# Softmax layers of a six-layer fp32 block on one core: copies moved ahead of exponents, filler and split positions changed, some low parts moved to GpSimd

## The reference, cut to what matters

```python
def dsa_mixer(xn, positions, w_in, q_norm, k_norm, w_out):      # the sparse layer
    q, k, v, z, qi, ki, wi = split(xn @ w_in)
    q = rope(rmsnorm(q, q_norm)); k = rope(rmsnorm(k, k_norm))  # 16 heads of 64
    rel = relu(einsum("qhd,sd->qhs", qi, ki)); score = einsum("qh,qhs->qs", wi, rel)
    top_val, top_idx = top_k(where(chunk_visible, score, -inf), 64)
    p = softmax(q . k[top_idx] * 64 ** -0.5)
    return ((p . v[top_idx]) * silu(z)) @ w_out

def mla_mixer(...):                                             # the latent layer
    cq, ckv, kr, z = split(xn @ w_in)
    q = rmsnorm(rmsnorm(cq) @ w_uq); kv = rmsnorm(ckv) @ w_ukv  # 16 heads of 96
    o = softmax over visible chunks (q . k * 96 ** -0.5) . v
    return (o * silu(z)) @ w_out
```

## Time and profile before

| what | us |
|---|---|
| median of 3 runs | 994.96 |
| lowest, highest | 992.82, 998.03 |
| profiled execution | 992.32 |
| its span, first to last instruction | 990.5 |
| PE busy within the span | 925.2 |
| DVE, ACT, POOL busy | 640.2, 500.1, 313.5 |
| mean granted TensorE clock | 0.974 |

### The profile page before, as it was taken

One profiled execution on the slowest core, in us unless ns is written; L12 is line 12 of the kernel. 1 busy time (PEld: TensorE's weight loads), 2 busy tenths in 40 slices (PEclk: granted clock), 3 DMA queues, 4 the chain that ended last, 5 costly groups with the idle time before them and its releaser, 6 DMA issues.

```text
span 990.5 us, 16827 instructions
## 1 busy us (share of the span) xinstructions
PE 925.2 (93%) x6793; PEld 867.7 (88%) x6793; DVE 640.2 (65%) x1006; ACT 500.1 (50%) x700; POOL 313.5 (32%) x270
## 2 busy tenths in 40 slices
PE   5999999988878997989999999899999999999988
PEld 5999987668667986769999999899999998988987
DVE  5776665896574788864677666678556544655642
ACT  5534455454574676674443353434535336575632
POOL 6433322342013225122443336965203000223320
PEclk9999999998999998999999999899999999999998
DMA  9886444344014425316386444253663752424401
GB/s 248 207 208 192 159 170 170 107 149 170 31 58 144 168 66 186 115 41 170 110 231 191 170 171 155 101 204 136 255 218 126 246 185 86 167 89 171 170 1 43
DMA packets 123170, 148.20 MB, mean 150 GB/s; under 512 B 9521, under 2 KB 79070, under 8 KB 123102
## 3 DMA queue, kind: packets, MB, share of 16 engines
q1 hardware_dynamic: 122384, 146.16, 45.6%
q0 software_dynamic: 464, 1.02, 0.4%
q10 hardware_dynamic: 254, 0.07, 0.0%
HBM read 146.18 MB, written 1.05 MB: 149 GB/s over the span
## 4 chain that ended last, share of the span: by engine, by line
PE 60%; DVE 8%; ACT 7%; POOL 3%; issue 2%; DVEq 0%; ACTq 0%; POOLq 0%
PE acc L1618 43%; PE aux L1618 16%; DVE wlo L862 2%; ACT whi L464 1%; POOL arena L1473 1%; ACT work L657 1%; ACT arena L490 1%; POOL arena L1474 1%; POOL arena L1472 1%; ACT whi L456 1%; ACT work L664 1%; ACT work L655 1%; DVE score L1110 1%; DVE arena L969 1%; DVE top L1109 1%
## 5 line engine op out<-in xcount | busy, mean ns | idle before, releaser
L862 DVE TENSOR_TENSOR wlo<-raw,whi 128x2048 fp32r<-128x2048 f32 (+5 forms) x118 | 281.3, 2410 | 104.2 <-ACT whi L456 102.5
L1618 PE MATMUL acc<-xh,whi 128*128 128x256 f32 x1128 | 323.7, 287 | 7.7 <-DVE wlo L862 4.2
L1618 PE MATMUL acc<-xl,whi 128*128 128x256 f32 x1128 | 320.9, 285 | 0.0
L1618 PE MATMUL acc<-xh,wlo 128*128 128x256 f32 x1128 | 320.8, 284 | 0.0
L456 ACT ACTIVATE whi<-raw 128x2048 fp32r<-128x2048 f32 (+5 forms) x118 | 202.9, 1748 | 86.5 <-PE aux L1618 45.3
L1618 PEld LDWEIGHTS acc<-xh,whi 128*128 128x128 f32 x1128 | 218.0, 193 | 9.9 <-issue 5.8
L1618 PEld LDWEIGHTS acc<-xl,whi 128*128 128x128 f32 x1128 | 218.1, 193 | 0.0
L1618 PEld LDWEIGHTS acc<-xh,wlo 128*128 128x128 f32 x1128 | 217.8, 193 | 0.0
L1618 PE MATMUL acc<-whi,xh 128*128 128x512 f32 (+1 forms) x208 | 82.6, 397 | 7.9 <-DVE arena L969 4.0
L1537 POOL CAST yh<-ytmp 128x256 fp32r<-128x256 f32 x24 | 16.9, 705 | 217.4 <-DVE ytmp L1393 123.3
L1618 PE MATMUL aux<-yh,whi 128*128 128x256 f32 x288 | 81.9, 284 | 0.0
(11 more groups left out here) (331 smaller groups left out, 1757.2 us busy)
## 6 DMA issues: line engine op xcount, KB each, us to landing
raw<-in_a_w_in SPq DMA_DIRECT2D x52, 512.0 KB, 6.7
raw<-in_sb_w_in SPq DMA_DIRECT2D x48, 512.0 KB, 5.6
raw<-in_b_w_in SPq DMA_DIRECT2D x36, 512.0 KB, 5.4
raw<-in_pool_w_in SPq DMA_DIRECT2D x32, 512.0 KB, 5.7
raw<-in_a_w_out SPq DMA_DIRECT2D x16, 512.0 KB, 4.9
raw<-in_pool_w_out SPq DMA_DIRECT2D x16, 512.0 KB, 5.1
raw<-in_sb_w_out SPq DMA_DIRECT2D x16, 512.0 KB, 5.0
raw<-in_a_w_in SPq DMA_DIRECT2D x16, 256.0 KB, 5.6
```

The lines of the kernel that those rows point to most:

```text
L862: TT(wlo[b][:, lo:hi], (raw_third if third else raw[b])[:, lo:hi], whi[b][:, lo:hi].bitcast(F32), ALU.subtract).then_inc(lo_ready, 1)
L1618: return nc.tensor.matmul(out_, lhsT, rhs, start=start, stop=stop, skip_group_check=True)
```

## The change

Ten edits, in the sparse and the latent layer.

- `root(1)` uses logarithm and exponent (`log=True`) in place of a square root, and B0+2's first half is split in two quarters on ACT and on DVE, with the root between ACT's quarters.
- DVE's second `top64` moves behind `half_factor(1)`, just ahead of `take(B0 + 7, ...)`.
- The low part of B0+8 moves from DVE (two halves) to POOL (four quarters, `weights_low`). POOL scales the last two k rows (rope 8 and 9) only after that; ACT splits B0+8 around `half_root(1)`.
- ACT copies transposed heads in pairs, at odd steps, ahead of that step's exponents.
- Filler positions: B0+9 at 5, 7, 8, 9 (were 6 to 9), C0+7 at 5, 7, 8, 9 (were 5, 6, 8, 9).
- C0+7 is split by quarters at steps 2 to 5, C0+8 at 8 to 11 (was 2 to 5), C0+9 at 12 to 15 (was 11 to 14).
- The table load inside `softmax_heads` is made once, ahead of the sparse layer's call.
- `turn_heads(15)` goes to psum bank acc 0, which the first PV uses; that PV waits for `turn_copy(15)`.
- In the q loop ACT's `log_root` for k stands ahead of the squares, and DVE's split of C0+5 and C0+6 behind the sums of c = 0 and c = 1.
- DVE's `turn_copy` 5 to 11 stand ahead of `q_factor(0)`.

```diff
-        MLA_SPLITS = {first + q: (u, q) for first, u in ((2, C0 + 8), (11, C0 + 9)) for q in range(4)}
+        MLA_SPLITS = {first + q: (u, q) for first, u in ((2, C0 + 7), (8, C0 + 8), (12, C0 + 9)) for q in range(4)}
...
-            return (acc[:, 1, :], acc[:, 2, :], acc[:, 3, :], acc[:, 1, :])[i - 12]
+            return (acc[:, 1, :], acc[:, 2, :], acc[:, 3, :], acc[:, 0, :])[i - 12]
...
-            split(B0 + 2, (0,))
+            split_quarter(B0 + 2, 0)
+            root(1, log=True)
+            split_quarter(B0 + 2, 1)
...
+            split(B0 + 8, (0,))
             half_root(1)
+            split(B0 + 8, (1,))
             token_out(3)
-            split(B0 + 8)
...
+                    if i % 2 and i > 1:
+                        for h in (i - 3, i - 2):
+                            act.wait_ge(sem("pt_psum"), h0 + h + 1)
+                            if h >= 2:
+                                act.wait_ge(sem("pv_done"), h0 + h - 1)
+                            A(work[:, 2 + h % 2, :], aux[:, 2 + h % 2, 0:W384], ACT.Copy)\
+                                .then_inc(sem("pt_ready"), 1)
                     if i < HEADS:
...
-                    if 2 <= i <= HEADS + 1:
-                        h = i - 2
...
-            split(C0 + 7)
             softmax_heads(1)
...
-            top64(P, W384)
             split(B0 + 7, (0,))
             token_turn(4)
             token_sums(4)
             half_mean(1)
             split(B0 + 7, (1,))
             half_factor(1)
-            split(B0 + 8)
+            top64(P, W384)
             take(B0 + 7, 24, "z_raw")
...
+            def weights_low(u, q, signal):
+
+                c = slice(1024 * q, 1024 * q + 1024)
+                pool.wait_ge(hi_ready, 2 * u + 1 + q // 2)
+                TT(wlo[u % 2][:, c], raw[u % 2][:, c], whi[u % 2][:, c].bitcast(F32), ALU.subtract).then_inc(signal, 1)
+
             for j in range(10):
                 token_rope(j)
+            pool.wait_ge(lo_ready, 2 * (B0 + 8))
+            for q in range(4):
+                weights_low(B0 + 8, q, lo_ready if q % 2 else sem("low_quarter"))
+            pool.wait_ge(sem("k_turned"), 2)
+            pool.wait_ge(sem("hfB_ready"), 2)
+            for j in (8, 9):
+                f = hf[:, 1, 1, HEADS * (j % 2) + 8:HEADS * (j % 2) + 16]
+                TT(by_head(raw_slot(j)), by_head(raw_slot(j)), f.rearrange("p (h d) -> p h d", d=1).broadcast_to([P, 8, 64]),
+                   ALU.mult).then_inc(sem("tok_done"), 1)
...
-                if 6 <= f < 10:
-                    if f == 6:
+                if f in (5, 7, 8, 9):
+                    if f == 5:
                         taken("v_ready", 4)
-                    unit(B0 + 9, in_tiles(1), xh, xl, part=(2 * (f - 6), 2))
+                    unit(B0 + 9, in_tiles(1), xh, xl, part=(2 * (5, 7, 8, 9).index(f), 2))
...
-                    unit(C0 + 7, in_tiles(1), xh, xl, part=(2 * (5, 6, 8, 9).index(f), 2))
+                    unit(C0 + 7, in_tiles(1), xh, xl, part=(2 * (5, 7, 8, 9).index(f), 2))
...
+                        if layer == 1 and t == 0:
+                            taken("turn_out_v", 8)
```

More of the change, by code:

```diff
@@ L547, in _ @@
             split(B0 + 1)
-            root(1)
             nc.scalar.preload_act_table_set("natural_log_exp_and_others")
@@ L677, in softmax_heads @@
                         nc.scalar.preload_act_table_set("natural_log_exp_and_others")
+            nc.scalar.preload_act_table_set("natural_log_exp_and_others")
             softmax_heads(0)
@@ L755, in _ @@
                 A(qraw[2 * g][:, h:h + 4, :], src, ACT.Copy).then_inc(sem("q_out_a"), 1)
+                if c == 0:
+                    log_root(c_heads(0, 1, 1), c_heads(1, 1, 1), "k_ms", 2, "k_root")
                 for t in range(NT):
@@ L1024, in _ @@
             split(B0 + 1)
-            factor(1, spread=False)
-            split(B0 + 2, (0,))
+            factor(1, spread=False, log=True)
+            split_quarter(B0 + 2, 0)
+            split_quarter(B0 + 2, 1)
             dve.wait_ge(sem("tab_ready"), 12)
@@ L1167, in softmax_heads @@
                         ins.then_inc(sem("p_ready"), 1)
+                    if layer == 0 and i == 4:
+                        dve.wait_ge(lo_ready, 2 * (B0 + 8) + 2)
                     if layer == 0 and i - 2 in SPARSE_SPLITS and i - 2 < 14:
@@ L1173, in softmax_heads @@
                         q_factor(1)
-                    if layer == 1 and i - 2 in MLA_SPLITS and i - 2 < 13:
+                    if layer == 1 and i - 2 in MLA_SPLITS and i - 2 < 14:
                         split_quarter(*MLA_SPLITS[i - 2])
+            dve.wait_ge(sem("picked"), 2)
             softmax_heads(0, pick, 24)
@@ L1265, in _ @@
                     ins.then_inc(sem("k_ms"), 1)
-            split(C0 + 5)
             for c in range(4):
@@ L1284, in _ @@
                     TS(c_heads(0, 0, g), c_heads(0, 0, g), 1 / 96, EPS, ALU.mult, ALU.add).then_inc(sem("q_ms"), 1)
-                if c == 1:
-                    split(C0 + 6)
+                if c < 2:
+                    split(C0 + 5 + c)
                 if c == 2:
@@ L1289, in _ @@
                     turn_copy(3)
+            for i in range(5, 13, 2):
+                turn_copy(i)
             q_factor(0)
-            turn_copy(5)
-            turn_copy(7)
-            turn_copy(9)
-            turn_copy(11)
-            split(C0 + 7)
             softmax_heads(1, mask, 40)
@@ L1522, in token_rope @@
                 ins = TT(raw, raw, turn, ALU.add)
-                if e in (2, 4):
-                    g = e // 2 - 1
+                if e == 4:
+                    ins.then_inc(sem("k_turned"), 1)
+                    return
+                if e == 2:
+                    g = 0
                     me.link(ins)
@@ L1544, in attention_low @@
                     if t in (4, 5):
-                        c = slice(1024 * (t - 2), 1024 * (t - 2) + 1024)
-                        pool.wait_ge(hi_ready, 2 * u + 2)
-                        TT(wlo[u % 2][:, c], raw[u % 2][:, c], whi[u % 2][:, c].bitcast(F32), ALU.subtract)\
-                            .then_inc(lo_ready if t == 5 else sem("low_quarter"), 1)
+                        weights_low(u, t - 2, lo_ready if t == 5 else sem("low_quarter"))
             pool.wait_ge(sem("turned"), 10)
@@ L1898, in mla_filler @@
                     turn_heads(13 + 2 * f)
-                if f in (5, 6, 8, 9):
+                if f in (5, 7, 8, 9):
                     if f == 5:
```

5 lines of the change are left out of this document (1 added, 4 removed).

## The result

The changed kernel takes **1000.3 us** (median of 8 runs, 999.3 to 1001.5); the kernel before, on the same chip, 994.7 (8 runs, 990.8 to 998.0). The ratio is 1.0058, with a 95% interval of 1.0039 to 1.0077: slower by 5.6 us, where 994.4, a range from 984.5 to 1000.0 and "no change" were forecast. The profiled execution of after has a span of 999.3 us and a time of 1001.45.

A forecast was written before the change was run, and what follows sets the result against it. PE was taken as busy nearly throughout, the two softmax stretches as chains between engines. Terms -3.3 + 5.9 - 1.0 - 2.2 gave -0.6 us, so the median went from 994.96 to 994.4, range 984.5 to 1000.0.

The forecast's parts named there:

- A: Start of B0+2: PE starts 1.7 us earlier and the clock is kept, 1.6 us more; -3.3, bounds -3.3 and -1.7.
- B: B0+7 and B0+8: first gap goes, but POOL's quarters delay DVE's half_factor, top64 and take; +5.9, bounds -5.1 and +6.5.
- C: Sparse softmax, from PE's first filler to the output product: -1.0 us, bounds -2 and +1.5.
- worse case: Sparse filler 5: the clock falls in PE's wait, so the transposes of pair 2 come at 269.4 instead of 268.1.
- D: Latent layer: first logits 5.5 us sooner, partly lost at filler 5 and to ACT; -2.2, bounds -4 and +1.9.
- low case: Latent filler 5 half at the low clock: scores of pair 3 at 406.8 instead of 405.3, giving -0.7.
- That order is unchanged: End of sparse softmax: ACT's last high quarter, POOL's 2.38 us, its two parts, gate and last PV still follow in turn.
- Rival 3: Both softmax layers: filler 5's 24 matmuls at 1.2 GHz delay needed scores; sum +5.0, median 1000.0 to 1001.6; chance 0.14.

The follow-up runs named there:

- e9: The kernel before with only the new start of B0+2 (root by logarithm and exponential, split by quarters): 992.1 us, ratio 0.9987.
- e12: Changed kernel with GpSimd's quarters behind half_factor, both fillers at 6, GpSimd's later low quarters, take within top64, but the old B0+2 start: 975.4 us, 0.9810 of before.
- e1: Changed kernel with GpSimd's four low quarters of B0+8 waiting until VectorE has finished half_factor: 992.7 us, 0.9985 of before.
- e2: Changed kernel with the four parts of B0+9 at sparse filler steps 6 to 9 instead of 5, 7, 8, 9: 996.6 us, 1.0020 of before.
- e3: Changed kernel with the four parts of C0+7 at latent filler steps 6 to 9 instead of 5, 7, 8, 9: 997.7 us, 1.0023 of before.
- e6: Changed kernel with the old copy order, each head's copy behind the exponents of the head two later: 1001.7 us, 1.0086 of before.
- e5: The kernel before with only the pair copies, ScalarE copying two heads ahead of the next exponents in both softmax layers: 992.2 us, ratio 0.9977.

## Why the prediction was wrong

**A, the start of B0+2: as forecast in the trace.** The gap is 1.76 (1.7 was forecast) and the clock is kept, so -1.5 and -1.6 against -3.3. The traces of e9 and e12 bear out the place, B0+8 coming 1.6 us sooner with the new start; in time they measured 0.6 us and 1.7 to 2.6, neither clear of noise.

**B, B0+7 and B0+8: right in mechanism and size.** +5.4 against +5.9: a gap of 12.54 us against "about 13", and four operations that pass one per quarter, the choice made between one and two. That the gap ahead of B0+7 goes is right as well (0.97). What the term left out is the clock behind the long gap: +1.2 us up to "turned". The rule of the Trainium skill that stands behind it, "SBUF — State Buffer", section "🔬 SBUF: two separate sides", is that the port pair of these two engines is locked for a whole instruction and not shared. The trace agrees where DVE's operation is a tensor_scalar or scalar_tensor_tensor (2.3 us instead of 0.2), and e1 shows maxima and replaces untouched.

**C, the sparse softmax: the step that failed.** Up to filler 5 all of it held. Counted from "turned" (252.64 in the frame of the prediction), PE was to arrive at filler 5 after 7.1 us and did after 7.0 (268.16 less the wait of 3.83, less 257.32); the low quarter was to be ready after 10.7 and PE started after 10.8. What failed is the clock behind that wait. The prediction's worse case had half the filler at 1.2 GHz, 1.3 us, with the transposes of pair 2 at 269.4, or 16.8 after "turned". All 24 matmuls ran at that level, 5.34 us where full clock gives 2.9, and the transposes came at 275.16, 17.8 after. The second failure is what such a delay is worth: the prediction compared the transposes with those of before (16.3) and called it even, since ScalarE's count was to bound the rest. In e2, without filler 5, they come 14.9 after "turned" (271.04 less 256.15) and the last PV 3.5 us sooner than in the changed kernel: the delay of 2.9 at pair 2 passes to the end whole. C was to be -1.0, with +1.5 as its bound, and is +1.6; e2 has -1.9. The filler, taken as nearly nothing, cost 3.5. What the prediction said of the end held: POOL's low quarter behind ACT's last high quarter starts 1.6 us later after "turned" than before (51.41 against 49.77 us), and the last PV comes 1.6 later. In e2 that quarter starts 47.87 us behind "turned", 3.5 sooner. So ACT's chain depends on when PE gives the scores, where the prediction counted ACT's own work alone.

**D, the latent layer: the same choice.** The front part came true: first logits 6.2 us sooner behind the event (27.02 against 33.26 us), 5.5 forecast. The prediction had two values, -2.2 for a filler at full clock and -0.7 at the low one, and took the first "since PE is denser there". The granted clock was 0.63 over 410 to 414.5 us, the scores of pair 3 come 46.2 us behind the event (46.4 in the low case), and D is -0.6. Here the low clock held for 14 of the 24 matmuls, near the half that the low case assumed. e3 has -4.3 against before, past the lower bound of -4.

**What stood in no step: the gate.** "That order is unchanged" was said of the chain over POOL's quarter to the last PV, and it was unchanged; but POOL's quarter came 1.6 us later after "turned" and PE only 0.6 later (52.53 us against 51.96), so the wait grew from 2.04 to 3.08 us in the sparse layer. In the latent layer it grew from 0.63 to 3.09, as the splits of C0+9 had moved from steps 11 to 14 to 12 to 15, which the prediction did not follow to POOL's quarter: with the moved splits and the old copies (e6) the wait there is 2.04, with the pair copies and the old splits (e5) 0.58. Behind each the clock fell: +1.5 twice, with no term in the sum.

With C at its upper bound and D at its low-clock value the forecast's own sum would have been +3.4 (-3.3, +5.9, +1.5, -0.7); the clock behind the gaps, 1.2 at B0+8 and 1.5 at each last PV, which had no term, makes it +7.6. Between the two profiled executions +7.5 was measured, the 1.2 us from the conv layer left out. The medians differ by 5.6 only. The forecast added to its sum the 2.6 us by which the profiled execution of before lay below its median, as if the changed kernel spread in the same way; its profiled execution lies 1.1 above its median. Which gaps made the other runs of before slower was not traced.

Rival 3 of the prediction named this mechanism: filler 5 ahead of scores that are needed, at the low clock, "over 3 us behind the transposes of pair 1". The waits were 3.83 and 3.24 us. That its median, 1000.0 to 1001.6, also holds the measured 1000.3 is luck. Its terms add up to +6.0 (-3.3, +5.9, +1.5, +1.9) and not to the +5.0 that it states, so the median should have been 1001.0 or more; D was -0.6 where it had +1.9, and the clock behind the gaps, 4.2 us in all, was in none of its terms. It was given 0.14, though the forecast's own C and D already had both waits in them: the difference was the clock level of 24 matmuls behind a wait of 3 to 4 us. For D the choice rested on "since PE is denser there". The one row read for a clock that is kept (idle for 1.84 of 5 us in several gaps) was used for A; its longest single wait is 1.75 us.

## What to carry to other kernels

In each of the two layers here, a filler ahead of work that others wait for cost about 3.5 us. It is only free if its own input is surely there: put it one step later rather than one earlier. Before moving an operation to GpSimd, look what VectorE has at that very time; here small dependent operations paid one whole GpSimd instruction each, max and match_replace nothing. At the end of a pipeline, look for a slow bulk piece in the same queue ahead of a short piece on the chain, and swap them: that needed one changed number here and gained 6.8 us.

## What was not expected of the hardware

- Small operations of VectorE beside back-to-back GpSimd quarters got exactly one passage per quarter: 2.26 to 2.33 us each instead of 0.17 to 0.19.
- GpSimd's quarter took 2.35 us each beside VectorE's maxima and replaces and beside the blocked operations alike; neither slowed it.
- The same gap of 2.04 us ahead of the last PV was followed by the high clock in some profiled executions and by the low one in others, 1.5 us apart. At that place gaps of about 0.6 us kept the clock in all of them but one, those of 3.1 us in none. The one is e5's latent layer: a wait of 2.47 us ended 0.6 us ahead of the gap of 0.58, and the stretch behind took 33.16 us instead of 30.48. Behind the same wait of 3.83 us the 24 matmuls of filler 5 took 5.3 us in the changed kernel and 4.4 in e6, where the first nine ran at full clock. Even one of 1.67 us, ahead of the scores of pair 3, was followed by 0.93 us for eight matmuls in before and by 1.65 in e2. So what a gap costs isn't read from its length alone. On one chip the kernel before, with gaps of 2.0 to 4.2 us, spread over 990.8 to 998.0 us, the changed one over 999.3 to 1001.5. Why the changed kernel, with more such gaps, spreads less was not tried.
